# One inference step of a two-layer hybrid decoder: the products of a weight block ordered bank by bank instead of pass by pass

## The reference, cut to what matters

```python
for layer in range(DEPTH):                       # DEPTH = 2
    h = rms_norm(x, norm_mix[layer])
    z = h @ w_in                                 # 1024 -> 3080 (layer 0), 2568 (layer 1)
    ...                                          # conv | attention, or mLSTM | pooling
    x = x + concat([a, b]) @ w_out               # 1024 -> 1024
    h = rms_norm(x, norm_ffn[layer])
    g, u = split(h @ w_up[layer])                # 1024 -> 2 x 2816
    x = x + (silu(conv(g) + conv_b) * u) @ w_down[layer]   # 2816 -> 1024
```

## Time and profile before

| | |
|---|---|
| median of 3 runs | 2711.54 us (2709.87 to 2715.56) |
| the profiled execution, its own time | 2715.68 us |
| span, first to last instruction | 2713.8 us |
| mean granted TensorE clock | 0.973 |
| TensorE busy (matmuls / weight loads) | 2582.8 / 2465.2 us |
| DVE, ACT, POOL busy | 1222.8, 670.7, 885.3 us |

### The profile page before, as it was taken

One profiled execution on the slowest core, in us unless ns is written; L12 is line 12 of the kernel. 1 busy time (PEld: TensorE's weight loads), 2 busy tenths in 40 slices (PEclk: granted clock), 3 DMA queues, 4 the chain that ended last, 5 costly groups with the idle time before them and its releaser, 6 DMA issues.

```text
span 2713.8 us, 41413 instructions
## 1 busy us (share of the span) xinstructions
PE 2582.8 (95%) x16810; PEld 2465.2 (91%) x16810; DVE 1222.8 (45%) x1491; ACT 670.7 (25%) x942; POOL 885.3 (33%) x554
## 2 busy tenths in 40 slices
PE   5999978999999999999998999879999999999996
PEld 4999955659999999999997999879999999999996
DVE  5988885442533333333336203162533333333335
ACT  4311244541411111111123222221321111111121
POOL 2766641002333333333332212242333333333330
PEclk9999988999999999999998999989999999999998
DMA  3877788982111111111111213312111111111111
GB/s 142 293 278 256 268 290 308 334 305 100 43 44 47 46 46 46 46 46 46 46 53 32 106 40 62 130 51 102 39 47 46 46 46 46 46 46 46 46 42 63
DMA packets 122774, 282.87 MB, mean 104 GB/s; under 512 B 20101, under 2 KB 24070, under 8 KB 122154
## 3 DMA queue, kind: packets, MB, share of 16 engines
q1 hardware_dynamic: 86218, 168.75, 17.7%
q10 hardware_dynamic: 36160, 111.61, 13.6%
q0 software_dynamic: 288, 1.05, 0.1%
HBM read 261.27 MB, written 20.07 MB: 104 GB/s over the span
## 4 chain that ended last, share of the span: by engine, by line
PE 77%; DVE 11%; DMA 4%; issue 3%; ACT 2%; SPq 2%; POOL 1%; POOLq 0%; DVEq 0%; ACTq 0%
PE G L756 64%; DVE KTMP L1884 3%; PE G L808 2%; DMA XT<-in_ck 2%; DVE XT L1867 2%; PE G L846 2%; PE M L969 2%; PE G L1116 1%; SPq L641 1%; PE M L1061 1%; PE G L1010 1%; DVE QT L1828 1%; PE G L1038 1%; DVE HLO L1815 0%; PE M L1204 0%
## 5 line engine op out<-in xcount | busy, mean ns | idle before, releaser
L2354 POOL TENSOR_TENSOR WLO<-WRAW,WHI 128x1024 fp32r<-128x1024 f32 x192 | 465.0, 2427 | 1287.3 <-ACT WHI L1633 834.0
L756 PE MATMUL G<-HHI,WHI 128*128 128x344 f32 x3312 | 709.3, 323 | 13.9 <-DVE XT L1941 5.0
L756 PE MATMUL G<-HLO,WHI 128*128 128x344 f32 x3312 | 705.7, 321 | 0.0
L756 PE MATMUL G<-HHI,WLO 128*128 128x344 f32 x3312 | 701.9, 320 | 0.0
L756 PEld LDWEIGHTS G<-HHI,WHI 128*128 128x128 f32 x3312 | 559.2, 189 | 17.6 <-issue 14.7
L756 PEld LDWEIGHTS G<-HLO,WHI 128*128 128x128 f32 x3312 | 563.4, 190 | 0.0
L756 PEld LDWEIGHTS G<-HHI,WLO 128*128 128x128 f32 x3312 | 554.5, 189 | 0.0
L2101 DVE TENSOR_TENSOR XT<-XT,G 128x1032 f32<-128x1032 f32 x172 | 211.5, 1230 | 349.0 <-PE G L756 348.7
L1633 ACT ACTIVATE WHI<-WRAW 128x1024 fp32r<-128x1024 f32 x108 | 112.3, 1056 | 494.0 <-PE G L756 494.0
L756 PE MATMUL G<-HIDH,WHI 128*128 128x344 f32 x960 | 204.4, 321 | 0.0
L756 PE MATMUL G<-HIDL,WHI 128*128 128x344 f32 x960 | 202.9, 320 | 0.0
(11 more groups left out here) (332 smaller groups left out, 2771.8 us busy)
## 6 DMA issues: line engine op xcount, KB each, us to landing
WRAW<-in_w ACTq DMA_DIRECT2D x192, 512.0 KB, 3.6
XT<-in_ck SPq DMA_DIRECT2D x256, 256.0 KB, 4.7
HF<-in_cv SPq DMA_DIRECT2D x176, 256.0 KB, 4.6
XT<-in_cv SPq DMA_DIRECT2D x80, 256.0 KB, 4.4
XT<-in_xp SPq DMA_DIRECT2D x2, 4096.0 KB, 17.0
x_scr<-XT SPq DMA_DIRECT2D x1, 4128.0 KB, 12.2
XT<-x_scr SPq DMA_DIRECT2D x1, 4128.0 KB, 13.5
out_y<-XT SPq DMA_DIRECT2D x2, 1376.0 KB, 5.4
```

The costliest lines, as they stand in the source:

```text
L756: mm = pe.matmul(out[:, c], w, x[:, c * TC:(c + 1) * TC], start=first and n == 0, stop=last and n == 2)
L2354: TT(WLO[:, s], WRAW[:, s], WHI[:, s].bitcast(F32), ALU.subtract).then_inc(w_lo, 1)
```

## The change: what it does

The two loops in `passes` change places: for each bank the three passes, then the next bank. The same 9 products are made with the same operands; bank 0 gets its three, then bank 1, then bank 2. The sum in each element of PSUM is made in the same order of passes as before. `start` and `stop` still go with the first and third pass, and the last product, whose instruction `passes` returns, is still the third pass into bank 2.

```diff
             def passes(out, whi, wlo, xhi, xlo, first, last):
 
-                for n, (w, x) in enumerate(((whi, xhi), (whi, xlo), (wlo, xhi))):
-                    for c in range(BANKS):
+                for c in range(BANKS):
+                    for n, (w, x) in enumerate(((whi, xhi), (whi, xlo), (wlo, xhi))):
                         mm = pe.matmul(out[:, c], w, x[:, c * TC:(c + 1) * TC], start=first and n == 0,
                                        stop=last and n == 2)
                 return mm
```

## The result

The changed kernel takes 2702.91 us (median, 2698.74 to 2706.55), the kernel before beside it 2713.62; the ratio is 0.9957 with a 95% interval of 0.9946 to 0.9967. That is 0.43% or some 11 us faster, where 4.9 us were forecast.

A forecast was written before the change was run, and what follows sets the result against it. TensorE's step between L756 products was taken as the bound from the attention on; (157.4 - 157.84) ns x 11160 products = -4.9 us, from 2711.54 to 2706.6 us. Range: -9.5 to +5.5 us, 2702 to 2717.

The forecast's parts named there:

- Where the time is: L756 products in MLPs and projections set the time, 157.83 ns each, 11160 on the path; before 346 us priced at nothing.
- Nothing added, no wait moved: In `passes`: no instruction added or removed, still 16810 loads for 16810 products, no wait moves; no cost in the sum.
- (a): Three products in a row into one bank in `passes`: costs nothing that shows; bank-by-bank `last_pair` 157.2 ns, `triple` 157.5 and 157.1.
- The rival of the turn of the bank: Turning to next bank, third and weights after the third pass becomes dear: slower, +5.1 us at 158.3 ns; chance 0.15.
- the one that made bank changes the cause of the 14 ns: Changing banks between L756 products makes 157.8 out of 143.3 ns; two of three changes gone gives -108 us; chance 0.03.
- (b): Block 6 of each unit reading HLO: 25 ns at its bank changes should go, 111 units, 2.8 us.
- (c): All other steps between L756 products: not derivable, taken as 157.4 against 157.84 ns; -4.9 us over 11160, the 2.8 included.
- Order-blind: Rival for the step between L756 products: pace ignores the loop order, total 2711.5 us, within 1 us; chance 0.22.
- Chances: Odds for the whole kernel's measured time against a 0.2% line: faster 0.37, same 0.51, slower 0.12.

## Why the prediction was right or wrong

*Where the time is.* Right: TensorE's step in the MLPs and projections. Nothing shows of a gain before 346 us, though up to 2 us couldn't be told there. I also read the chain up to 409 us as free of TensorE; it has 8 products of L969, 1.10 us at 396.81, but none of L756.

*Nothing added, no wait moved.* Right: 16810 loads, the other engines as busy as before. Had a block been loaded once and used repeatedly, as the Trainium skill (TensorE: Matmul & The Clock Gate, "Step-by-step: what each phase is for") describes it, the change would have added loads; here each product had its load before and after, and the trace shows no loss.

*(a) The same bank again is free.* Right, and more than that: the bank has no part in it. Turning the bank at every product leaves 700.69 us. The rival of the turn of the bank is refuted with it, and so is the one that made bank changes the cause of the 14 ns.

*(b) The dear spot.* It is gone, as foreseen, but that its 25 ns a unit are a gain by themselves is not so: with 128 free bytes it is gone too, and the units still take 157.8 ns. The steps it was made of are handed on; only the mean of a whole run of reads is a price. The count was off as well: an MLP has 42 such units (3024 / 72), not 40, so 115 on the path. The 2.8 us stood within the 4.9, so the forecast doesn't hang on it.

*(c) All other steps: this is the step that failed.* I took 157.4 ns, "nearest to `triple`", and it is 156.67 for units and 157.42 for `down`, 156.97 on the mean of 4464 (700.69 / 4464). The term of the sum is then (156.97 - 157.84) x 11160 = -9.7 us instead of -4.9; counted by kind, 8280 products in units and 2880 in `down`, it is -10.3. The span shows -9.9, but that is partly chance: outside the MLPs it has 1.2 us that the order doesn't explain, and 1.1 us lost before them. The mechanism, what is read after what, was right; its size was borrowed from code with the same banks but another run of reads. Alone on TensorE, a unit in the manner of `last_pair` has 157.4 (L474) and the new order 156.7. Shared banks made L846, L808 and L1116 look like neighbours, and banks don't matter. The bound of 156.7 was among the rows, from 24 products of L1116; nothing shows that it is there for the same reason. That 2702.91 lies inside the range is luck: it is 8.6 under the 2711.54 I started from, but the kernel before was itself some 2 us slower over more runs, and the change, 10.7 us or 0.43%, is over double the forecast and beyond the 9.5 us at which the range ended.

*Order-blind.* Refuted in the units, nearly true in `down` (157.62 to 157.42). The formula of the Trainium skill (same page, "Back-to-back issue gap") for a matmul without a stream of loads, columns at 2.4 GHz and 2.5 ns, gives 146 ns; no row of 344 columns here, each product with its load, has under 153.3.

*Chances.* Half of the chance lay on no measurable change, because the estimate lay at 0.18% against a line at 0.2%.

## What to carry to other kernels

When products follow each other without a wait, a loop order can be worth half a percent without moving a wait, and what counted here is the run of read addresses, not the bank or the weight block. A price for it can't be borrowed from other code with the same shape: run the intended order alone on TensorE, which gave the whole kernel's pace to 0.1 ns in a few hundred products. If high and low parts of an operand are read in turn, try their distance in steps of 32 bytes as well as the order. And don't price one dear step by itself: it can go while the mean stays.

## What the runs showed of the hardware

A 128x128 product with 344 columns, with its weight load, at a granted clock of 1.00 took 153.3 to 160 ns. With one read address it went by where the read begins modulo 256 bytes (160 at +160, 155.6 at +224); with changing reads by which follow each other (156.7 and 157.8 with low and high parts 0 or 128 bytes apart); and by what ran before, for equal products held 153.3 or 157.8 ns over 90 to 180 of them. Where all reads begin at one place the place of the weights seems to count too (157.8 and 160.0), but there it was not separated from what ran before. Read from one address, 256 to 384 and 512 columns cost their time at 2.4 GHz plus 13.3 to 14.4 ns, 448 columns 19.8. Why 256 bytes, and what the two paces are, no run here settles. In the kernel, turning the bank at every product changed nothing (700.69 us twice); alone, an accumulation that starts anew and a repeated weight block changed nothing within 0.2 ns, though one row of 48 with advancing reads took 7.59 us with turning banks and 7.57 without. The other engines' work made no difference above 0.1 ns: 156.7 and 157.8 ns alone as in the kernel.
